# Two changes to a four-layer kernel: a merged second-layer input block, and more expert blocks in the gate table stage

## The reference

```python
c_a, c_b, c_g, d_q, d_kv, d_bg, d_g, m_q, m_g = split_cols(h @ w_in, ODD_SPLITS)   # 1024 x 3864
y_c = silu(rms_norm(causal_conv31(c_a * sigmoid(c_b)) + conv_b, norm_g)) * silu(c_g)
q = rope_partial(rms_norm(q, qnorm)); ks, kw = the same with knorm      # 8 heads of 64, 2 key groups
kc = compress(k_cmp_raw)      # blocks of 32 tokens at stride 16: 15 of them; (flat + pos) @ w1, silu, @ w2
kc = rope_partial(rms_norm(kc, knorm), cmp_end); vc = compress(v_cmp_raw)
y_d = compressed, selected and window attention, mixed by gates; y_m = memory attention
```

```python
act = gelu(einsum('bcd,bchkd->bchk', hc, u_tab[ic]))
out = einsum('bchk,bchkd->bcd', gc * act, v_tab[ic])
```

## Time and profile before

| | us |
|---|---|
| median of 3 runs | 2776.42 |
| lowest to highest | 2776.33 to 2778.36 |
| profiled execution, its own time | 2776.5 |
| its span | 2774.8 |

### The profile page before, as it was taken

How to read it: one execution, slowest core, us unless ns; L and a number is a source line. 1 busy time by engine, 2 the same in 40 slices (tenths; PEclk the granted TensorE clock), 3 DMA queues, 4 the chain that set the end, 5 groups by cost and what they waited for, 6 DMA issues and landing times. The chain is left out here.

```text
span 2774.8 us, 39291 instructions
## 1 busy us (share of the span) xinstructions
PE 2401.8 (87%) x11693; PEld 1958.9 (71%) x11693; DVE 1993.0 (72%) x4652; ACT 1163.1 (42%) x2042; POOL 149.7 (5%) x166
## 2 busy tenths in 40 slices
PE   4797882885588899999999995779889999999996
PEld 3576442754477778888888873567768888888885
DVE  3668186626679878888888873659987777777775
ACT  3566111510413854444444432441574444444443
POOL 0000000000013500000000000001430000000000
PEclk9899995897799999999999997889999999999998
DMA  6341440046222056777777753121115555555553
GB/s 218 129 167 48 156 154 30 7 160 237 86 74 77 0 185 239 255 254 255 250 257 254 253 181 134 61 76 62 61 46 190 195 186 192 191 187 195 185 195 106
DMA packets 145041, 429.23 MB, mean 155 GB/s; under 512 B 15380, under 2 KB 21809, under 8 KB 144945
## 3 DMA queue, kind: packets, MB, share of 16 engines
q1 hardware_dynamic: 144944, 428.14, 44.6%
HBM read 427.05 MB, written 1.05 MB: 154 GB/s over the span
## 5 line engine op out<-in xcount | busy, mean ns | idle before, releaser
L2433 PE MATMUL bank<-h_t_parts,u_t_high 128*128 128x512 f32 x1888 | 466.5, 389 | 0.1
L2433 PEld LDWEIGHTS bank<-h_t_parts,u_t_high 128*128 128x128 f32 x1888 | 354.4, 188 | 73.9 <-DVE u_t_low L2541 0.5
L2506 ACT ACTIVATE u_t_high<-u_ring 128x1024 fp32r<-128x1024 f32 x236 | 250.5, 1062 | 189.6 <-DMA u_ring<-in_peer_u 186.2
L2447 PE MATMUL bank<-v_high,weighted_high 128*128 128x512 f32 x992 | 311.1, 395 | 9.6 <-DVE weighted_low L2566 7.4
L2541 DVE TENSOR_TENSOR u_t_low<-u_ring,u_t_high 128x1024 fp32r<-128x1024 f32 x236 | 288.5, 1223 | 29.5 <-ACT u_t_high L2506 26.1
L2447 PE MATMUL bank<-v_low,weighted_high 128*128 128x512 f32 x992 | 309.2, 393 | 0.0
L2447 PE MATMUL bank<-v_high,weighted_low 128*128 128x512 f32 x992 | 308.0, 392 | 0.0
L2526 ACT ACTIVATE activated<-activated 128x256 f32<-128x256 f32 x236 | 99.0, 420 | 492.1 <-DVE activated L2554 492.1
L2548 DVE TENSOR_TENSOR v_low<-v_ring,v_high 128x1024 fp32r<-128x1024 f32 x248 | 301.6, 1216 | 4.0 <-PE bank L2454 2.7
L2513 ACT ACTIVATE v_high<-v_ring 128x1024 fp32r<-128x1024 f32 x248 | 261.2, 1053 | 43.6 <-PE bank L2447 41.9
L2436 PEld LDWEIGHTS bank<-h_t_parts,u_t_low 128*128 128x128 f32 x1888 | 257.6, 190 | 18.4
(11 more groups left out here) (588 smaller groups left out, 3778.5 us busy)
## 6 DMA issues: line engine op xcount, KB each, us to landing
v_ring<-in_peer_v SPq DMA_DIRECT2D x248, 512.0 KB, 3.7
u_ring<-in_peer_u SPq DMA_DIRECT2D x236, 512.0 KB, 4.6
panel<-in_l_w_in SPq DMA_DIRECT2D x15, 2048.0 KB, 8.0
late_tiles<-in_ada_w SPq DMA_DIRECT2D x54, 512.0 KB, 4.6
mod_ring<-in_ada_w SPq DMA_DIRECT2D x42, 512.0 KB, 5.2
panel<-in_peer_w_q SPq DMA_DIRECT2D x8, 2048.0 KB, 7.9
panel<-in_l_w_out SPq DMA_DIRECT2D x4, 2560.0 KB, 9.0
early_u<-in_peer_u SPq DMA_DIRECT2D x20, 512.0 KB, 3.6
```

Source lines behind the costliest of these rows:

```text
L2433: nc.tensor.matmul(banks[2 + k][:, :], UTH[:, k, j, :], H2[:, j, :, :].rearrange("p a s -> p (a s)"), start=(j == 0), stop=False, skip_gro ...
L2447: last = nc.tensor.matmul(banks[4 + 2 * t + half][:, :], w[:, t * P:(t + 1) * P], v[:, k, half * 512:(half + 1) * 512], start=False, stop= ...
L2506: nc.scalar.activation(UTH[:, s, :, :].rearrange("p a b -> p (a b)"), UR[:, s, :], ACT.Copy)\
```

## The change

**Second layer.** One hand-written block, `odd_input`, takes the place of nine stages. The panels are multiplied in another order (query and key columns early, the gate of the convolution last), and the compression's panel comes between the sixth and the seventh. PE has further work between groups: the transposes of the gated input behind group 4, of the raw keys behind 8, the compression behind 11, the second compression layer behind 12, query and key transposes behind 14, the rest and the convolution's result behind 15. ACT evacuates all groups and takes over the squares, the doubling of the raw keys and all copies out of PSUM. DVE has the taps in six parts (14, 3, 2, 3, 2 and 7), with operand additions (now 8 instructions), norms and rotations between them. Both token tiles go in one instruction. PE waits for all small loads first (`small_loaded`). The position vectors come transposed from the host, and the query heads are reordered by the host so that two key groups share a transposed tile; the doubled copies of keys disappear.

**Experts.** `EARLY` becomes 14. The query stage still makes 10 blocks (`ROUTED`). The other 4 are made in the gate table stage: PE has one f32 product of 256 columns behind each of the first 32 steps, SP loads four u blocks into a ring of two (`UG`), ACT copies four results. PE's stream is unrolled, ACT's for 36 steps. The first v blocks are loaded after the last of these products, since they lie where h lies. `DEEP` becomes 12; the row of c is loaded in the expert loop and activated at block 10. Both layers have this.

```diff
-    pn["odd_in"] = wide(I["l1_w_in"], KD, ODD_IN)
+    ODD_PANELS = ((0, 512), (512, 512), (1536, 512), (2048, 512), (2560, 512), (3352, 512), (3072, 280), (1024, 512))
+    odd_panels = lambda some: [panel([rows_by_k(I["l1_w_in"], KD, n0, n)], 2) for n0, n in some]
...
+    pn["odd_in"] += odd_panels(ODD_PANELS[6:])
...
-    EARLY = 10
+    EARLY, ROUTED = 14, 10
...
+    load_early.append((cgain[:, :], bcast(I["l1_c_norm"])))
...
+            @block.sync
+            def _(sp):
+                issue_early(sp)
+                for p in range(ps[0], ps[-1] + 1):
+                    load_panels(sp, p + 3)
...
+                    if j == 4:
+                        for t in range(NT):
...
+                    if j == 8:
+                        pe.wait_ge(raw_doubled, 2 * NT)
...
+                    if j == 11:
+                        wait_panel(pe, pc)
+                        pe.wait_ge(operand_ready, 8)
+                        pe.wait_ge(conv_in, NT)
...
+                    if j == 12:
+                        pe.wait_ge(acc_free["a"], hidden_done)
+                        pe.wait_ge(raw_copied, 2)
...
+                    if j == 14:
+                        pe.wait_ge(normed[0], 6)
...
+                        pe.wait_ge(k_cmp_copied, 1)
...
+                    if j == 15:
+                        pe.wait_ge(normed[1], 3)
+                        pe.wait_ge(v_cmp_stored, 1)
...
+                        pe.wait_ge(conv_done, 1)
+                        pe.wait_ge(q_copied, NT)
...
+                pe.wait_ge(small_loaded, v0)
+                for i, p in enumerate(ps):
+                    n = ODD_PANELS[i][1]
+                    w = slots[p % 3][:, 0:KD * n].rearrange("p (k n) -> p k n", k=KD)
+                    wait_panel(pe, p)
+                    for t in range(NT):
+                        j = 2 * i + t
+                        wait_acc_free(pe, group(j))
+                        for k in range(KD):
+                            last = nc.tensor.matmul(acc_bank(group(j))[:, 0:n], HT[:, k, t * P:(t + 1) * P], w[:, k, :],
+                                                    start=(k == 0), stop=(k == KD - 1))
+                        last.then_inc(acc_ready, 1)
+                        beside(j)
...
+                evac(0, 1, 2, 3, 4)
+                act.wait_ge(cleared_d, 1)
...
+                evac(5)
+                squares(0, 1536, 512, 0, 5)
+                evac(6, 7)
+                act.wait_ge(acc_free["a"], evacuated(7))
+                for t in range(NT):
+                    for i in range(2):
+                        a = 2048 + i * P
+                        nc.scalar.activation(RAW2[:, t, i, :, :, :], P1[:, t, a:a + P].rearrange("p (g d) -> p g d", d=HD)
+                                             .unsqueeze(2).broadcast_to([P, D_GROUPS, 2, HD]), ACT.Copy).then_inc(raw_doubled, 1)
+                squares(0, K_SLC, P, 1024, 7)
+                evac(8)
+                for i in range(2):
+                    act.wait_ge(raw_turned, i + 1)
+                    nc.scalar.activation(RT[:, i, :, :].rearrange("p g s -> p (g s)"), banks[4 + i][:, :], ACT.Copy)\
+                        .then_inc(raw_copied, 1)
+                evac(9)
+                squares(0, K_WIN, P, 1280, 9)
...
+                evac(10)
+                root(0, COLS0)
+                evac(11)
+                squares(1, M_Q, 256, 0, 11)
...
+                evac(12)
+                act.wait_ge(k_cmp_done, 1)
...
+                act.wait_ge(k_cmp_copied, 1)
+                nc.scalar.activation(room[0:N_CMP, 512:512 + P], KC[:, :, :].rearrange("p g d -> p (g d)"), ACT.Square)\
+                    .then_inc(squared[1], 1)
+                evac(13)
+                root(1, COLS1)
+                evac(14)
...
+                dve.wait_ge(conv_in, NT)
+                conv(0, 14)
+                for i in range(2):
+                    dve.wait_ge(raw_copied, i + 1)
...
+                            ks = slice(late * CMP_K // 2, (late + 1) * CMP_K // 2)
+                            f(v.tensor_tensor(OP[r, i, ks, :, :], steps[:, odd::2, :, late:late + N_CMP],
+                                              POST[r, i, ks].unsqueeze(2).unsqueeze(3)
+                                              .broadcast_to([HD, CMP_K // 2, D_GROUPS, N_CMP]), ALU.add),
+                              operand_ready, wait=False)
+                conv(14, 17)
+                dve.wait_ge(squared[0], 3)
...
+                means(COLS0, HD, mean_done[0])
+                conv(17, 19)
+                dve.wait_ge(root_done[0], 1)
+                inverse(COLS0)
...
+                conv(19, 22)
+
+                dve.wait_ge(squared[1], 2)
+                f(v.tensor_reduce(ss[:, 0, M_COL:M_COL + 8], room[:, 0:512].rearrange("p (g d) -> p g d", d=HD), AX.X, ALU.add),
...
+                means(COLS1, HD, mean_done[1])
+                dve.wait_ge(v_cmp_done, 1)
...
+                conv(22, 24)
+                dve.wait_ge(root_done[1], 1)
+                inverse(COLS1)
...
+                conv(24, C_KERNEL)
+
+                cols = slice(C_SUM, C_SUM + NT)
+                dve.wait_ge(conv_squared, NT)
+                f(v.tensor_scalar(ss[:, 0, cols], ss[:, 0, cols], 1.0 / 512, EPS, ALU.mult, ALU.add), conv_mean, wait=False)
+                dve.wait_ge(conv_root, 1)
+                inverse(cols)
+                ready()
+                for t in range(NT):
+                    dve.wait_ge(conv_copied, t + 1)
...
+                    for n in range(EARLY - ROUTED):
+                        if n >= 2:
+                            sp.wait_ge(table_acted, n - 1)
+                        sp.dma_start(UG[:, n % 2, :], I["peer_u_2"][l][(ROUTED + n) * P:(ROUTED + n + 1) * P, :])\
+                            .then_inc(table_u[n % 2], 16)
+                    sp.wait_ge(table_acted, EARLY - ROUTED)
...
-                    for s in range(R4):
-                        step(s, s)
-                    with pe.Fori(1, S // 16) as i:
-                        for s in range(R4):
...
+                    for n in range(S // 4):
+                        step(n, n % R4)
+                        b, k = divmod(n, KD)
+                        if b < EARLY - ROUTED:
+                            if k == 0:
+                                pe.wait_ge(table_u[b % 2], 16 * (b // 2) + 16)
+                                if b >= 2:
+                                    pe.wait_ge(table_copied, b - 1)
+                            last = nc.tensor.matmul(banks[6 + b % 2][:, 0:S], UG[:, b % 2, k * P:(k + 1) * P], HT[:, k, :],
+                                                    start=(k == 0), stop=(k == KD - 1))
+                            if k == KD - 1:
+                                last.then_inc(table_acted, 1)
...
+                    def copy_table(n):
+                        act.wait_ge(table_acted, n + 1)
+                        nc.scalar.activation(ACTED[:, ROUTED + n, :], banks[6 + n % 2][:, 0:S], ACT.Copy).then_inc(table_copied, 1)
...
+                    unrolled = KD * (EARLY - ROUTED) + R4
+                    for n in range(1, unrolled):
+                        gate(n, n % R4)
+                        store(n - 1, (n - 1) % R4)
+                        if n > KD and n % KD == 1:
+                            copy_table(n // KD - 1)
+                    with act.Fori(unrolled // R4, S // 16) as i:
```

More of the change, by code:

```diff
@@ L1651, in cmp_dve @@
                     for odd in range(2):
                         r = slice(HD * odd, HD * odd + HD)
-                        first = 2 * k + odd
-                        f(nc.vector.tensor_scalar(OP[r, i, k, :, :], RT[r, i, :, first:first + span:CMP_STRIDE],
-                                                  POST[r, i, k:k + 1], None, ALU.add), operand_ready, wait=False)
-            dve.wait_ge(acc_free["a"], owners[:g0 + 2].count("a"))
-            for g in range(D_GROUPS):
-                f(nc.vector.tensor_copy(HIDV[:, 4 * g:4 * g + 4, 0:N_CMP],
-                                        HID[:, 1, g, :].unsqueeze(1).broadcast_to([P, 4, N_CMP])), hidden_spread, wait=False)
@@ new lines, in _ @@
+                ready()
+                cos, sin = (rc[0:N_CMP, 8 * i:8 * i + 8].unsqueeze(1).broadcast_to([N_CMP, D_GROUPS, half]) for i in range(2))
+                tmp = [room[0:N_CMP, 640 + i * 16:656 + i * 16].rearrange("p (g h) -> p g h", h=half) for i in range(4)]
+                x1, x2 = KC[:, :, 0:half], KC[:, :, half:2 * half]
+                for out, x, y in ((tmp[0], x1, cos), (tmp[1], x2, sin), (tmp[2], x1, sin), (tmp[3], x2, cos)):
+                    f(v.tensor_tensor(out, x, y, ALU.mult), wait=False)
```

470 lines of the change are left out of this document (293 added, 177 removed).

## The result

| | us |
|---|---|
| changed kernel, median of 4 runs | 2705.68 (2703.25 to 2707.28) |
| kernel before, same chip, median of 4 runs | 2777.14 (2776.33 to 2778.36) |
| ratio, 95% interval | 0.9742 (0.9725 to 0.9758) |
| span of the profiled execution | 2701.5 (before 2774.8) |

What follows compares the result with a forecast made beforehand. Bounds: PE's projection, then exposed convolution and small serial stages; ACT and DVE in the gate table stage; PE in the expert loop. 2776.5 - 44.4 (merged block) - 14.8 (experts) = 2717.3 us; range 2703 to 2731, with unknowns and rivals 2700 to 2742.

Steps and rivals of the forecast that it cites:

- Late start: Head of the merged block: PE waits for all small loads, the last gain vector landing last; 8.4 us.
- Compression products: Merged block, PE behind group 11: the compression matmuls take 14.1 us, as when they stood alone before.
- Group 12: Merged block, PE's projection group of 280 columns behind the compression products; 3.75 us.
- Stalls: Merged block: DVE waits 7.2 us for the raw keys, then 9.0 us for the compressed keys' square.
- Tail: End of the merged block: convolution transposes, ACT copies and squares, then norm, scale and product; block ends at 137 us.
- at most 0.06 a step; I count nothing: Gate table stage: register work that unrolled loops lose on ACT and PE, priced at nothing.
- Start: First steps of the gate table stage: half-speed PE and late first table rows put PE 1.4 us back.
- ACT's copies: Gate table stage: four copies of finished blocks at 0.38 us on ACT, 1.5 us a layer.
- The products themselves: Gate table stage: one f32 product in each of 32 steps, nearly covered; 0.02 us a step, 0.6 in all.
- Merged but not interleaved: First rival, merged block: DVE stalls twice the forecast size, norm work behind the projection; 16.3 us more, 2734; 16%.
- PE as the bound of the gate table stage: Second rival: PE holds the gate table steps, 0.3 us more in each of 32, twice; 19 us, 2737; 13%.
- A clock that stays at 1.2 GHz: Third rival: half clock through the gate table stage's first 32 steps, 2.58 us a step; 2791, slower than before; 3%.

Runs made afterwards that it cites:

- Experiment 3: Changed kernel with PE's wait for the small loads moved from the head of the projection to group 12; 2697.53 us, ratio 0.9717.
- Experiment 10: Kernel before, plus nine products of no use on PE while DVE makes the first compression operands; 2776.42 us, ratio 0.9997.
- 21.9 alone: Kernel before with only the expert change (four more early blocks in both layers), second layer as before; 2755.96 us, ratio 0.9922.
- experiment 6: Kernel before with PE's and ACT's gate table loops both written out, no table products, no block moved; 2771.06 us, ratio 0.998.
- experiment 12: Kernel before with only ACT's gate table loop written out for its first 36 steps; 2771.91 us, ratio 0.9982.
- experiment 5: Changed kernel with each of the 32 table products of a gate table stage made twice, second into a spare bank; 2732.49 us, ratio 0.9849.
- experiment 9: Changed kernel with the small-load wait moved to group 12 and table products on steps 4 to 35 instead of 0 to 31; 2701.5 us, ratio 0.9719.
- Experiments 8: Changed kernel with the small-load wait moved to group 12 and DVE's two stalls filled with convolution taps; 2697.97 us, ratio 0.9716.

## Why the prediction was right, and where it was off

**Right in place, wrong in size, in the merged block: 52.1 against 44.4 us.** Point by point:
- *Late start:* 8.4 predicted. Against the old start it is 7.15, in idle time of PE 7.8 (8.79 less the 0.97 that stood there before), by the load that was named. Experiment 3 shows that it lay on the path: 8.2 us by the medians, 5.1 at the start of attention in the traces.
- *Compression products:* 14.1 predicted, 8.16 measured. This is the failed term, 5.9 us too dear. I took 2 x 7.04 from the earlier trace rows, rows of a PE that had idled and ran at a granted clock of 0.50, and put it into a PE that is never idle. In the changed kernel the clock is 0.87 over the same work (389 to 398). Experiment 10 shows rate and clock fall together. I had read the granted clock of about a half in the seventh slice as a weakness of the kernel before, and not as the reason for a duration that I was about to use.
- *Group 12:* 3.75 predicted, 6.38 measured (397.56 to 403.94), a miss the other way that I had no term for. The clock falls during the compression products and is at its lower level for most of the group behind them; group 13 took 3.83. So 2.6 of the 5.9 us go back, and the compressed keys' squares reach DVE 4.7 us earlier than forecast (405.02, 101.2 on the block's clock, for 105.9). These 4.7, 0.8 in DVE's work behind them and 1.0 in the tail and border make up the 6.5 us by which the block was shorter than its 137.5; the rest of the 7.7 is the late start.
- *Stalls:* 7.2 and 9.0 predicted, 5.8 and 6.8 measured. The first is shorter since ACT needs 2.0 us for group 8 (368.31 to 370.34, with one table load) and not my 3.5 with two, the second since the compressed keys came earlier with the products.
- *Operand additions:* 3.2 predicted for a range of 2.2 to 17.4; 4.2 measured, swallowed by the second stall as the text had it.
- *Order of the end:* convolution last by about 2 us; PE waits 1.85 us. PE's own stream ends at 120.4 on the block's clock instead of 125.3, less by the 4.8 that it had won by the end of the compressed keys' products.
- *Tail:* two table loads, at 429.13 and 430.64:

```profile
429.13 1.28 ACT L1762 ACT_TABLE_LOAD   x1
430.42 0.20 ACT L1762 ACTIVATE sums<-sums 128x2 f32<-128x2 f32 x1
430.64 1.28 ACT L1765 ACT_TABLE_LOAD   x1
432.43 1.29 ACT L1765 ACTIVATE conv_out<-conv_out 128x512 f32<-128x512 f32 x2 [0.51 <-DVE conv_out L1896]
```

The activation stands 1.29 us behind the start of the first load, and the second load lies beside DVE's inverse. The drain of 1.38 us of the Trainium skill (ScalarE: Activation LUTs, What ACT_TABLE_LOAD costs) isn't in these rows either, as it wasn't in the earlier trace rows.

**The experts: 21.9 alone against 14.8.** The saving per block held: 10.5 and 12.5 us a layer for 10.9, the second with a clock of 0.91 in the first 20 us of the loop where the kernel before had 0.83. What failed is one sentence, that the unrolled loops lose "at most 0.06 a step; I count nothing". Experiments 6 and 12 put it at 3.2 and 1.7 us of the two stages, 5.2 us of the time. Against the unrolled stage without products (86.9 and 86.8 us) the four blocks cost 2.8 and 3.2 us, near my 3.5. Its split held in the main. Start: 1.4 predicted; the first eight steps take 13.53 and 13.72 us against 12.13 in experiment 6, so 1.4 and 1.6. ACT's copies: 1.5 predicted for four; each of the first three makes two steps 1.47 and 1.40 us instead of 1.32, so 0.23 a copy and 0.7 in all; the fourth lies behind the last product, where no such pair shows. The products themselves: 1.32 a step against 1.30, the 0.02 that I had taken. The reason that I gave was wrong in one place: by the earlier trace rows I took ACT as the engine that holds the step, and with the loop written out it waits up to 0.4 us for PE's products in every second step of experiment 12, while DVE is busy for 19.86 of 20 us. With the products PE has 20.00 of 20.00. Two errors in the same direction, 7 us in each part, are what the range had to hold; it did by 5.7 us at its lower end (2700).

**The rivals.** Merged but not interleaved did not come: both stalls are below my sizes, and filling them gives 1.5 us in the trace. PE as the bound of the gate table stage came true as a fact (experiment 5: the next 0.43 us are paid whole), but without the 0.3 us a step that I had put behind it: a step with a product takes 1.32. My sum for it was 0.03 short, since PE's one-hots take 0.89 from start to start and not 0.86. What covered that was the step of the kernel before, 1.37 and 1.35 us on average, where I had read a single one of 1.32 in the earlier trace rows. A clock that stays at 1.2 GHz did not come: 1.00 in 849 to 869. The rule of the Trainium skill (TensorE: Matmul & The Clock Gate, What's actually happening), that activity releases the throttle, goes with that window. It doesn't go with the compression products, in which the clock fell from 1.00 to 0.50 while PE was busy for 9.00 of 9.00 us, and it doesn't tell why the clock behind the stage was lower in experiment 9.

**What stays open.** 1.1 us more between attention and the gate table stage, which may be nothing, since the same code takes 394.7 us there in the trace of experiment 3 and 398.3 in that of experiment 9; what sets how long the start of an expert loop runs at 1.2 GHz; and what brings the clock down within the compression products. No run prices the clearing of the added semaphores, which I had put at nothing.

The best kernel of these is the changed one with the wait moved (2697.53 us). Experiments 8 and 9 add nothing to it that can be measured.

## What to carry to other kernels

Before a duration is moved into a new place, read the granted clock over its own rows: the compression products had been priced at half speed, and in the merged block most of them ran at the full clock. Then read the rows behind it in the new place too, since the clock that these products brought down was paid by the group behind them. Take a wait to the group that needs its data, since at the head of this block it cost 7.8 us of idle PE, while idle time of an engine that isn't last is worth only what the last one waits for it. And when a change unrolls a loop, price the unrolling by itself, engine by engine; here it was a quarter of what its part gained.

## What was not expected of the hardware

Writing out ACT's loop of the gate table stage for 36 of 64 steps took 3.1 and 1.5 us off the stage, while writing out all of PE's took 0.3 off one and added 0.1 to the other. And PE's clock after a short pause is no function of the pause: the same 2.37 us before the first one-hot product, with the same instructions ahead of it, is followed by six instructions in 0.94 us in the changed kernel's third layer and in 1.65 us in its fourth. In the third the lower clock comes one step later: its first product takes 1.22 us (832.68), as it does in the fourth, where 0.60 is usual. Nor does PE have to be idle for the clock to fall: within the 64 compression instructions it fell with PE busy throughout.

```profile
830.55 0.94 PE L2551 MATMUL bank_pair<-onehot,onehot 128*128 128x128 f32 x6 [2.37 <-DVE onehot L2523]
```

```profile
1912.38 1.65 PE L2551 MATMUL bank_pair<-onehot,onehot 128*128 128x128 f32 x6 [2.37 <-DVE onehot L2523]
```
